# A decoder layer with a mixture of experts: a weight load of the third slot without its wait for the first gather

## The chip, the cores and the metric

The kernel runs on one core of a Trainium2 chip. The time is device microseconds of one execution: 581.81 us before, the median of 3 runs (579.86 to 581.87).

## What is computed

One decoder layer on 512 tokens of 1024 channels, in float32: an RMS norm and one input projection; a gated causal convolution (31 taps) beside block-sparse attention; an output projection; a hierarchical mixture of experts; a gate with per-layer embeddings, and a last norm. The part that matters here is the mixture. With x1 the state after the output projection:

```python
x = x + mixed @ w_out[i]                         # x1
g_idx = argmax(hf @ w_group + b_group)           # one of 4 groups for each token
top_vals, top_idx = top_k(e_logits, 2)           # two of its 8 experts
for e in range(32):
    hid = silu(h @ w_gate[e]) * (h @ w_up[e])    # 1024 -> 256
    y = y + gates[..., e:e + 1] * (hid @ w_down[e])
```

## The kernel before, in words

**Passes.** The 32 experts are worked in pairs, one pair to a pass. A pass takes 128 rows: 96 for its first expert (a = 0) and 32 for its second (a = 1). Passes 0 to 2 have fixed pairs (experts 2g and 2g + 1, `FIXED = 3`); the later ones are ordered by their number of tokens, which is known only after routing, and SyncE reads their experts' numbers from `order` in SBUF (`expert`, L579 to L583). GpSimd gathers a pass's rows from `rows_d` in DRAM into `xg` by an indirect DMA (L792 for passes 0 and 1, L772 for the others) and scatters its results to `y_d` (L786). Before that it stores the four quarters of the normed rows to `rows_d` (L761). In all its queue carries 4 stores, 17 gathers and 16 scatters. TensorE transposes the rows (`turn_tokens`, L1788), does the gate and up products (64 matmuls, L1800), transposes the hidden rows (L1813) and does the down products (32 matmuls, L1822). ScalarE and VectorE empty the banks in between (L968 to L981, L1371, L1449, L1454).

**Slots.** The weights of a pass are six loads of 1 MB: w_gate, w_up and w_down of each expert. There are three slots (`SLOTS = 3`): slots 0 and 1 lie in `wring`; slot 2 is put together from tiles that the earlier stages have given up: `mix` and parts of `arena` for gate and up, and, for the second expert's w_down, parts of the constants `c` and the tile `lnr`. Pass 3 would use slot 0 again; its first expert's gate and up are put "aside" in `xs`, the tile in which x1 was made, as soon as x1 is stored in DRAM (L686).

**SyncE's order around the change** (L619 to L695). All weight loads are issued by SyncE, on one queue, in the order of the program. Before and during the output projection it issues slot 0, most of slot 1 and parts of slot 2. After the last product of the output projection (`outc` 7) it loads the rest of slot 1, stores the last quarter of x1 (L650), and issues `load_one(2, 2, 0, 0)`, w_gate of slot 2's first expert. Then comes the wait for `gathered[0]`, the landing of pass 0's rows, then `load_one(2, 2, 1, 0)`, w_gate of slot 2's second expert, then the waits for the last root and for the logits' bank, and `load_split_rest(2)` into `lnr` (L609). Behind that stand the waits for the order ("owner"), for all stores of x1, and for the rows of the norm, and the two loads into `xs`. Then `reload` refills the slots: halves of gate and up after half of a pass's products (`half_up`, only for passes 0 and 1), the rest after `up_done`, w_down after `down_done`.

**TensorE around the first gather.** While VectorE works out the routing, TensorE runs filler transposes of the identity into a bank that nobody reads (`keep_busy`, L1732): 52, then 18, then 18. After the last 18 come `turn_tokens(0, 0, 0)`, which waits for `gathered[0]`, and pass 0. The gather itself waits for `tfirst`, the list of rows of passes 0 and 1 (L1348).

Of the kernel before, what the change touches and what calls it, by code (L numbers as in the profile page):

```python
# [215 lines left out]
def build(nc, x, w_in, w_out, w_r, w_gate, w_up, w_down, w_pg, w_pp, pT, b_pg, g_final, prm, cst, out):  # L216
    ctx = ExitStack()
    with ctx:
# [7 lines left out]
        def sem(name):  # L226
            return ctx.enter_context(nc.semaphore(name))
# [256 lines left out]
        gathered = [sem(f"gathered{s}") for s in range(2)]  # L484
# [47 lines left out]
        def _(sp):  # L532
# [52 lines left out]
            def load_one(w, n, a, i):  # L585
                sp.dma_start(up_w(w, a)[:, i],  # L586
                             (w_gate, w_up)[i][bass.ds(expert(n, a), 1)].rearrange("e (p k) n -> p (e k) n", k=DK)
                             ).then_inc(up_loaded[w], 16)
# [60 lines left out]
                banks.wait_emptied(sp, ("outc", 2 * TT - 2 + half))  # L649
            sp.dma_start(x1_rows[:, TT - 1], xs[:, TT - 1, :]).then_inc(x1_stored, 16)  # L650
            load_one(2, 2, 0, 0)
            sp.wait_ge(gathered[0], 16)
            load_one(2, 2, 1, 0)

            sp.wait_ge(root_ready, 4 * TT)
            banks.wait_emptied(sp, "logit")
            load_split_rest(2)
# [1260 lines left out]
```

## Time and profile before

| | |
|---|---|
| median of 3 runs | 581.81 us (579.86 to 581.87) |
| profiled execution, its own time | 579.72 us |
| its span | 577.9 us |
| mean granted TensorE clock | 0.958 |
| TensorE matmuls busy | 502.6 us (87%) |
| DMA read and written | 142.95 MB and 14.68 MB, 273 GB/s over the span |

A line is named as L586; a line can be that of a helper (`load_one` of SyncE is L586, whatever it loads, and a filler transpose is L1732). "SPq" is SyncE issuing DMAs; a DMA that is issued is not yet landed, and the time to landing stands apart. "A <- B" in a list of waits means that A's engine stood idle until B was done. In the windows, the DMA share is the mean busy share of the 16 DMA engines, and PEclk the TensorE clock granted, 1.00 being 2.4 GHz and 0.50 being 1.2 GHz.

### The profile page before, as it was taken

What the parts mean: (1) busy time and instruction counts of PE and PEld (TensorE: products, weight loads), DVE (VectorE), ACT (ScalarE), POOL (GpSimd) and SP (SyncE); (2) the same over time, 40 slices, a digit from 0 to 9 for tenths busy, and PEclk for the clock granted to TensorE, in tenths of its full rate; (3) what the DMA queues carried; (4) which work ended last, traced back from release to release, by engine and by line L of the source; (5) the groups of instructions that cost most, each with busy time, mean ns of one, the idle gap of its engine ahead of it and who ended that gap; (6) DMA issues with size and microseconds to landing.
All of it is one profiled execution on the core that took longest, in us unless ns stands there. A gap on an engine that the chain in (4) does not pass through costs nothing.

```text
span 577.9 us, 8877 instructions
## 1 busy us (share of the span) xinstructions
PE 502.6 (87%) x3227; PEld 298.8 (52%) x3227; DVE 295.7 (51%) x561; ACT 183.7 (32%) x351; POOL 78.5 (14%) x91
## 2 busy tenths in 40 slices
PE   3999999997879979988999996879868687999993
PEld 3788888774557658874333332223213222247882
DVE  4339899999996864487121111111101111166776
ACT  6821411337775353332011000000000000066764
POOL 1740000000032040010212221010111101010000
PEclk9999999999799999999999997997979899899998
DMA  9931300445506056498999999999999999868003
GB/s 315 372 134 39 113 15 16 149 159 170 218 1 273 1 216 258 160 388 306 356 410 416 419 418 421 417 419 420 380 412 409 387 375 414 341 223 317 0 9 139
DMA packets 38936, 150.33 MB, mean 260 GB/s; under 512 B 6000, under 2 KB 10608, under 8 KB 27888
## 3 DMA queue, kind: packets, MB, share of 16 engines
q1 hardware_dynamic: 33280, 139.14, 61.2%
q0 software_dynamic: 5328, 10.50, 5.0%
q8 instruction: 26, 0.43, 0.3%
q10 hardware_dynamic: 288, 0.15, 0.1%
q14 instruction: 14, 0.11, 0.1%
HBM read 142.95 MB, written 14.68 MB: 273 GB/s over the span
## 4 chain that ended last, share of the span: by engine, by line
PE 56%; SPq 15%; DMA 10%; DVE 9%; ACT 5%; issue 4%; POOL 1%; DVEq 0%; ACTq 0%; POOLq 0%
PE bank L1554 15%; PE bank L1800 10%; DMA wring<-w_up_in 8%; PE bank L1866 8%; SPq L586 7%; PE bank L1656 5%; PE bank L1822 4%; PE bank L1580 4%; SPq L514 3%; SPq L614 2%; PE bank L1845 2%; DMA wring<-w_in_in 2%; PE bank L1697 1%; DVE wring L1151 1%; DVE mix L1088 1%
## 5 line engine op out<-in xcount | busy, mean ns | idle before, releaser
L1800 PE MATMUL bank<-wring,arena 128*32 128x512 f32 x656 | 87.2, 657 | 20.7 <-DMA wring<-w_up_in 19.4
L1088 DVE SCALAR_TENSOR_TENSOR mix<-arena,pr,mix 128x512 f32<-128x512 f32 x120 | 86.6, 791 | 0.0
L1449 DVE TENSOR_TENSOR arena<-arena,bank 128x256 f32<-128x256 f32 x16 | 6.7, 420 | 139.1 <-ACT arena L975 139.1
L1800 PEld LDWEIGHTS bank<-wring,arena 128*32 128x32 f32 x656 | 25.0, 119 | 76.4 <-issue 71.1
L975 ACT ACTIVATE arena<-bank 128x256 f32<-128x256 f32 x16 | 6.2, 384 | 140.5 <-PE bank L1800 140.5
L1822 PE MATMUL bank<-wring,arena 128*32 128x512 f32 x352 | 40.0, 595 | 5.3 <-ACT arena L978 5.3
L1800 PE MATMUL bank<-mix,arena 128*32 128x512 f32 x240 | 37.7, 626 | 7.4 <-DMA arena<-w_up_in 7.4
L1454 DVE COPY arena<-bank 128x512 f32<-128x512 f32 x16 | 11.1, 692 | 53.7 <-PE bank L1822 53.7
L1800 PE MATMUL bank<-arena 128*32 128x512 f32 x80 | 37.6, 626 | 0.0
L1554 PE MATMUL bank<-hT_hi,win_hi 128*128 128x512 f32 x128 | 33.5, 398 | 2.1 <-DVE hT_lo L1066 1.5
L1554 PE MATMUL bank<-hT_lo,win_hi 128*128 128x512 f32 x128 | 31.6, 389 | 0.0
L1554 PE MATMUL bank<-hT_hi,win_lo 128*128 128x512 f32 x128 | 31.6, 389 | 0.0
L1554 PEld LDWEIGHTS bank<-hT_hi,win_hi 128*128 128x128 f32 x128 | 23.6, 188 | 10.3 <-ACT hT_hi L838 1.9
L981 ACT ACTIVATE arena<-bank 128x512 f32<-128x512 f32 x16 | 9.6, 597 | 60.8 <-PE bank L1822 60.8
L1800 PEld LDWEIGHTS bank<-mix,arena 128*32 128x32 f32 x240 | 10.7, 115 | 33.7 <-issue 31.6
L1554 PEld LDWEIGHTS bank<-hT_lo,win_hi 128*128 128x128 f32 x128 | 24.0, 188 | 5.0
L1554 PEld LDWEIGHTS bank<-hT_hi,win_lo 128*128 128x128 f32 x128 | 24.0, 188 | 5.0
L783 POOL COPY ycur<-tlist 128x1 int32 x16 | 2.9, 182 | 169.5 <-DVE arena L1454 169.5
L1822 PEld LDWEIGHTS bank<-wring,arena 128*32 128x32 f32 x352 | 10.3, 109 | 27.6 <-issue 20.5
L743 POOL TENSOR_TENSOR mixa_lo<-mix,mixa_hi 128x512 fp32r<-128x512 f32 x4 | 5.9, 1480 | 134.8 <-ACT mix L899 134.8
L1371 DVE TENSOR_TENSOR arena<-bank,pr 128x512 f32<-128x512 f32 x33 | 21.3, 686 | 2.0 <-PE bank L1788 1.9
L833 ACT ACTIVATE win_hi<-wring 128x1024 fp32r<-128x1024 f32 x20 | 20.0, 1070 | 6.3 <-DMA wring<-w_in_in 6.3
(262 smaller groups left out, 907.2 us busy)
## 6 DMA issues: line engine op xcount, KB each, us to landing
wring<-w_down_in SPq DMA_DIRECT2D x22, 1024.0 KB, 20.6
wring<-w_gate_in SPq DMA_DIRECT2D x18, 1024.0 KB, 16.1
wring<-w_up_in SPq DMA_DIRECT2D x18, 1024.0 KB, 19.9
wring<-w_in_in SPq DMA_DIRECT2D x3, 2048.0 KB, 14.4
arena<-w_down_in SPq DMA_DIRECT2D x5, 1024.0 KB
mix<-w_up_in SPq DMA_DIRECT2D x5, 1024.0 KB, 12.2
arena<-w_up_in SPq DMA_DIRECT2D x5, 1024.0 KB, 21.8
mix<-w_gate_in SPq DMA_DIRECT2D x5, 1024.0 KB, 17.4
```

The lines of the kernel that those rows point to most:

```text
L514: return eng.value_load(ap, min_val=least, max_val=most)
L586: sp.dma_start(up_w(w, a)[:, i], (w_gate, w_up)[i][bass.ds(expert(n, a), 1)].rearrange("e (p k) n -> p (e k) n", k=DK)).then_inc(up_loaded ...
L614: sp.dma_start(dn_w(w, a), src).then_inc(dn_loaded[w], 16)
L833: act.activation(win_hi[i][:, :, cols], win[i][:, :, cols], ACT.Copy).then_inc(win_hi_ready[i], 1)
L1088: ins = dve.scalar_tensor_tensor(out=mixc[:, mm, :], in0=u[:, mm, j:j + S], scalar=w, in1=mixc[:, mm, :], op0=ALU.mult, op1=ALU.add)
L1371: dve.tensor_tensor(xgT[:, s, 4 * kh:4 * kh + 4, :], pb[kh][:].rearrange("p (k n) -> p k n", k=4), pr[:, Q_FFN + 4 * kh:Q_FFN + 4 * kh + 4 ...
L1554: ins = pe.matmul(bk(name)[:], w[:, k, m * P:(m + 1) * P], h[:, k, :], start=(j == 0 and k == 0), stop=(j == 2 and k == DK - 1))
L1580: ins = pe.matmul(bk(("v", t))[:], h[:, k, t * P:(t + 1) * P], w[:, k, :], start=(j == 0 and k == 0), stop=(j == 2 and k == DK - 1))
L1656: ins = pe.matmul(bk(name)[:], src[:, m, t * P:(t + 1) * P], weight[:, m, half * 512:(half + 1) * 512], start=(j == 0), stop=(j == 3 * CM ...
L1800: ins = pe.matmul(pb[2 + s][lo:hi, :], xgT[:, s, k, lo:hi], weights[:, :, k, :], start=(k == 0), stop=(k == DK - 1))
L1822: ins = pe.matmul(pb[6 + half][lo:hi, :], hidT[:, s, k, lo:hi], dn_cols(w, a, k, half), start=(k == 0), stop=(k == FK - 1))
L1866: ins = pe.matmul(bk(name)[:], lhs, w[:, k, :], start=(j == 0 and k == 0), stop=(j == 2 and k == DK - 1))
```

## The change

SyncE no longer waits for pass 0's rows ahead of w_gate of slot 2's second expert. All else stays.

```diff
             sp.dma_start(x1_rows[:, TT - 1], xs[:, TT - 1, :]).then_inc(x1_stored, 16)
             load_one(2, 2, 0, 0)
-            sp.wait_ge(gathered[0], 16)
             load_one(2, 2, 1, 0)
-
             sp.wait_ge(root_ready, 4 * TT)
             banks.wait_emptied(sp, "logit")
             load_split_rest(2)
```

## Rows read from the trace of the kernel before

**Rows 1.** Chain that ended last, 240 to 300: start us, us, what.

```profile
258.69 3.37 PE bank L1732 x18
...
262.05 1.41 PE bank L1788 x8
...
264.68 7.07 PE bank L1800 x64
```

**Rows 2.** GpSimd's timeline at the first gather, then line L792 in 258 to 259.

```profile
258.09 1.07 POOL L792 DMA_INDIRECT arena<-rows_d,tfirst  x1 [10.53 <-DVE tfirst L1348]
...
DMA to landing us min/median/max: 3.7/3.7/3.7
```

**Rows 3.** SyncE's waits, 240 to 283: us in total, times, longest.

```profile
SPq L586 <- DMA arena<-rows_d,tfirst: 17.2, 1, 17.2
```

**Rows 4.** SyncE's timeline, 240 to 283: start us, us, what.

```profile
243.75 0.43 SPq L650 DMA_DIRECT2D x_d<-xs  x1
...
244.23 0.43 SPq L586 DMA_DIRECT2D mix<-w_gate_in  x1
...
261.84 0.33 SPq L586 DMA_DIRECT2D arena<-w_gate_in  x1
...
262.27 0.41 SPq L609 DMA_DIRECT2D lnr<-w_down_in  x1
...
263.94 0.35 SPq L686 DMA_DIRECT2D xs<-w_gate_in  x1
...
265.07 0.34 SPq L686 DMA_DIRECT2D xs<-w_up_in  x1
...
278.63 1.44 SPq L614 DMA_DIRECT2D wring<-w_down_in  x2
```

**Rows 5.** Windows: us, busy by engine, PEclk, DMA share, GB/s.

```profile
242.00:258.00 16.00, 13.57 (x133) 12.71 (x132) 10.98 (x48) 7.59 (x9) 0.53 (x1) 1.00 1.01 389
...
259.50:263.00 3.50, 3.50 (x19) 3.28 (x18) 2.93 (x13) 0.00 (x0) 0.98 (x1) 0.51 0.44 123
...
278.00:279.00 1.00, 1.00 (x16) 0.37 (x12) 0.54 (x1) 0.45 (x1) 0.04 (x1) 1.00 0.65 262
...
282.00:350.00 68.00, 64.82 (x580) 22.39 (x576) 14.40 (x28) 7.59 (x17) 13.19 (x21) 1.00 1.02 412
```

**Rows 6.** Line L650, the last store of x1 (issued at 243.75).

```profile
DMA to landing us min/median/max: 15.5/15.5/15.5
```

**Rows 7.** VectorE's timeline, 257 to 260.

```profile
258.46 0.17 DVE L1358 CAST order<-bank 1x32 int32<-1x32 f32 x1
```

**Rows 8.** Line L786 in 280 to 281, then in 290 to 500; last, L772 in 275 to 276.

```profile
L786 POOL DMA_INDIRECT y_d<-arena,ycur x1: 1011/1011/1011, 280.2 to 280.2; - x1
...
DMA to landing us min/median/max: 7.9/7.9/7.9
...
DMA to landing us min/median/max: 7.7/8.5/9.1
...
L772 POOL DMA_INDIRECT arena<-rows_d,tcur x1: 1017/1017/1017, 275.2 to 275.2; - x1
...
DMA to landing us min/median/max: 6.2/6.2/6.2
```

**Rows 9.** TensorE's timeline, after two pauses, and the window of the first.

```profile
458.78 9.79 PE L1800 MATMUL bank<-wring,arena 128*32 128x512 f32 x64 [3.95 <-DMA wring<-w_up_in]
...
490.98 8.77 PE L1800 MATMUL bank<-wring,arena 128*32 128x512 f32 x64 [2.95 <-DMA wring<-w_up_in]
...
458.50:464.00 5.50, 5.22 (x28) 1.48 (x32) 0.00 (x0) 0.00 (x0) 1.02 (x1) 0.50 1.00 414
```

**Rows 10.** Part 3 of the page, DMA queues.

```profile
q1 hardware_dynamic: 33280, 139.14, 61.2%
...
q0 software_dynamic: 5328, 10.50, 5.0%
```

## The prediction

> **What bounds the kernel now.** I read the chain of waits first, then SyncE's waits and issues around the changed line, then what the first gather and the DMA engines do there, and last how TensorE behaves after a pause. The profiled execution spans 577.9 us and took 579.72 us, 2.1 us under the median of 581.81; the sum is made against it, and its difference is then put on 581.81.
>
> The chain goes through the place where the removed wait sits. TensorE runs its last 18 filler transposes up to 262.05 and goes straight on to the transposes of pass 0's rows (L1788), then to its 64 gate and up products at 264.68, which take 7.07 us [rows 1]. So pass 0 lies on the path, and so do its rows. The first gather is issued at 258.09 and lands 3.7 us later, at 261.8 [rows 2]: only 0.25 us before the filler ends. There is no other slack: a gather that lands later than 262.05 delays pass 0 by the difference.
>
> SyncE stands in the removed wait for 17.2 us, "SPq L586 <- DMA arena<-rows_d,tfirst" [rows 3], and then issues four loads: w_gate of slot 2's second expert at 261.84, the end of that expert's w_down into `lnr` at 262.27, and the two loads into `xs` (w_gate and w_up of pass 3's first expert) at 263.94 and 265.07 [rows 4]. Nobody on the chain waits for any of them: pass 2 and pass 3 come much later, and the chain names TensorE for passes 0 and 1. What the wait does buy is in the windows: the DMA engines are full up to 258 (389 GB/s), and in 259.5 to 263 they move 123 GB/s at a share of 0.44 [rows 5]. That is the two gathers, nearly alone.
>
> **The change, part by part.** (1) One wait instruction goes from SyncE: nothing on any path by itself.
>
> (2) The w_gate load of 1.05 MB (1024 KB) moves from 261.84 to right behind the one issued at 244.23, so about 244.7. The 0.26 MB for `lnr` follows as soon as the logits are read. Neither has a register to read, since pass 2 is one of the fixed ones. The DMA queue is full there, so they move no byte earlier than the end of that queue. Before, the queue's last load is the one of 244.23. The x1 store ahead of it lands 15.5 us after 243.75, at 259.25 [rows 4, 6]; behind it come the 1.05 MB, 2.5 us at the 412 GB/s of the full stretch [rows 5]. With the two loads added, 1.31 MB / 412 GB/s = 3.2 us more of full queue lie behind them, just where the gather starts moving (258.09 plus its own 1.07 us of issue = 259.16 [rows 2]).
>
> (3) The two loads into `xs` are no longer held by the rows. They need the order, which VectorE writes at 258.46 [rows 7], and all x1 stores, the last of which lands at 259.25. Before, 1.26 us passed between the end of the `lnr` issue (262.68) and the first of them (263.94) [rows 4], for the waits, already met, and the register reads. So they go out at about 260.4 and 261.5, 3.5 us earlier, 2.1 MB more. Together with (2) SyncE's queue is then full through the whole life of both gathers.
>
> (4) What a gather costs under a full queue. The trace has it later: the scatter issued at 280.2, the same kind of transfer from the same queue, with nothing of GpSimd's ahead of it, between 2 MB of w_down issued from 278.63 and the loads after, lands after 7.9 us. The 14 later scatters take 7.7 to 9.1 us, median 8.5. The gather of 275.2, whose neighbours ran out on the way (share 0.65 in 278 to 279), took 6.2 us [rows 5, 8]. I take 7.9 us, since the load standing beside that one, 1 to 2 MB ahead and 1 MB coming, is closest; bounds are 3.7 us (no harm at all) and 9.1 us. Rows at 258.09 + 7.9 = 265.99 instead of 261.8, so pass 0 begins 265.99 - 262.05 = **3.9 us** later. The second gather, needed only after pass 0's products, stays hidden: even 9.1 us and 3 us more behind the first end before the 271.7 + 3.9 at which it is asked for.
>
> (5) TensorE now stands idle from 262.05 to 266.0. After pauses of 3.95 and 2.95 us before 458.78 and 490.98 the 64 products took 9.79 and 8.77 us instead of 7.07, and the granted clock was 0.50 (1.2 GHz of 2.4) in 458.5 to 464 [rows 1, 9]. Work at half clock loses half of its time, so 2 x (9.79 - 7.07) = 5.4 us and 2 x 1.7 = 3.4 us of these products ran at the low level. The transposes run at half clock before as well (0.51 in 259.5 to 263 [rows 5]) and cost nothing new. The products start 264.68 - 262.05 = 2.6 us after the transposes, so with the same stretches counted from the transposes 0.8 to 2.8 us of the products run low, cost 0.4 to 1.4; I take **0.9 us**. Bounds: 0, if the clock is high by then, and 2.7 us, the full price of 458.78.
>
> (6) Is any of it given back? By 278 to 279 the queue has run down before as well (share 0.65), and it fills again for good only with the w_down loads at 278.63, which wait for pass 0's last product. From 282 on it is full (1.02) [rows 4, 5]. So the bytes moved early only lengthen the pause before that point, and the start of the full stretch, on which both the TensorE part up to 350 and the DMA part behind it hang, moves with pass 0. Nothing comes back: gain 0, cover the pause at 278.
>
> Sum: 3.9 + 0.9 = **4.8 us** later, 579.7 + 4.8 = 584.5 for the profiled execution, 581.8 + 4.8 = **586.6 us** for the median. Bounds within this case: low, the gather at 6.2 us (264.3, 2.2 us late, no cost of clock), 584.0; high, 9.1 us (5.1 late) and 2.7 of clock, 589.6.
>
> **Rivals.** *A: the gather takes its turns and hardly suffers.* SyncE's queue moved 139.14 MB in 33280 packets, 4.2 KB each; GpSimd's queue 5328 packets over its 37 transfers, 144 each, 9 on each of 16 engines [rows 10]. One packet of 4.2 KB on one of 16 engines takes 4.2 KB x 16 / 412 GB/s = 0.16 us. If each packet of the gather waits for just one such, it loses 9 x 0.16 = 1.5 us, lands at 263.3 and costs 1.2 us: 583.0, no change. Against it stand the scatters of [rows 8], which lose over 4 us to 3.7 with that very traffic; for it, that the queue might be shorter at 259 than I think. The Trainium skill ("DMA: Bandwidth & Descriptors", Queues, rings and completion order) says that each DMA engine goes round robin between its queue rows, packet by packet, which is this mechanism; by that rule alone the time would be 583.0, while the trace's scatters speak against it being all. Chance 0.19.
>
> *B: faster.* The pause of 259.5 to 263 is filled with 1.31 MB that are then not in the later full stretch: 3.2 us less if the gather still lands by 262.05 and the queue never runs empty between 263 and 282. That gives 578.6, just over 0.5% less. It decides from the point where the bytes saved exceed the pause at 278; the share of 0.65 there is against it, as is [rows 8]. Chance 0.05.
>
> **How the numbers follow.** 0.5%, 2.9 us, is about what a measurement of this kernel can tell from no change. My case, a late gather, has 0.76, of which its low end (gather 6.2 us, under 2.9 us in all) falls within 0.5%: some 0.05. So faster 0.05, same 0.19 + 0.05 = 0.24, slower 0.71. The range takes in rival A's 583.0 with a little below it for the scatter of runs (579.86 to 581.87), and goes up to the high bound: 582 to 590.
>
> **What would show it.** In the profile after: the SyncE row for the wait gone, w_gate issued near 244.7 and the `xs` loads at 260 to 261; DMA share near 1.0 in 259.5 to 263 where it was 0.44; the first gather 7 to 9 us to landing instead of 3.7; a wait "PE L1788 <- DMA arena<-rows_d" of about 4 us; the granted clock low into pass 0's 64 products and these over 7.07 us; all later passes shifted by the same 4 to 5 us; DMA share well under 0.65 near 275 to 283. A gather that lands within 5.5 us makes me wrong towards A. Later passes that are shifted by less than pass 0 make step 6 wrong, and a shift that shrinks through the full stretch would be B's.

## The result, and the profile after

The changed kernel takes **586.62 us** (median of 5 runs, 585.4 to 587.69) against 581.81 us: slower, ratio 1.0091 with the 95% interval 1.0064 to 1.0117, so by 3.7 to 6.8 us. The profiled execution took 585.49 us, its span is 583.7 us against 577.9. Lines of the changed kernel are two lower than before behind the change: L1786 is L1788 of before, L1798 is L1800, L790 is L792.

SyncE's timeline of the changed kernel, start and duration in us:

```profile
245.91 0.44 SPq L586 DMA_DIRECT2D mix<-w_gate_in  x1
246.39 0.44 SPq L586 DMA_DIRECT2D arena<-w_gate_in  x1
248.88 0.33 SPq L609 DMA_DIRECT2D lnr<-w_down_in  x1
261.82 0.35 SPq L684 DMA_DIRECT2D xs<-w_gate_in  x1
262.96 0.34 SPq L684 DMA_DIRECT2D xs<-w_up_in  x1
284.56 1.44 SPq L614 DMA_DIRECT2D wring<-w_down_in  x2
```

The wait of 17.2 us is gone, and w_gate for `arena` leaves right behind the one for `mix`, where [rows 4] have it 17.6 us later. The rows that the change does not touch are 1.5 to 1.7 us later too (the `mix` load at 245.91 against 244.23, the first gather's issue at 259.57 against 258.09), and that is no effect of the change: it arises at 213, ahead of every instruction that it moves. The chain of before and then of after:

```profile
213.78 3.92 PE bank L1656 x16
```

```profile
213.39 5.79 PE bank L1654 x16
```

The same 16 matmuls began 0.4 us earlier and took 1.9 us more, since the granted clock was at its low level for a moment (0.50 in 212 to 215, where it was 1.00 before); that leaves 1.5 us. Two single executions differ by such things; so below, times inside a profile are counted from the issue of the first gather, 258.09 before and 259.57 after. In the chain of after this stretch reads:

```profile
259.57 6.45 DMA arena<-rows_d,tfirst
...
266.06 1.98 PE bank L1786 x8
...
269.26 8.42 PE bank L1798 x64
```

The chain now leads through the gather: 6.45 us to landing instead of 3.7 [rows 2]. The transposes of pass 0's rows begin 6.49 us after the issue (before 262.05 - 258.09 = 3.96), and the 64 products end 18.11 us after it (before 13.66, [rows 1, 2]): **4.4 us** later. TensorE's timeline gives the pause, and the windows the reason and the clock (columns as in [rows 5]):

```profile
266.06 1.97 PE L1786 MATMUL bank<-c,arena 128*128 128x128 f32 x8 [3.71 <-DMA arena<-rows_d,tfirst]
```

```profile
259.50:263.00 3.50, 2.40 (x20) 2.05 (x20) 3.15 (x13) 0.00 (x0) 2.08 (x2) 1.00 0.99 419
265.50:272.00 6.50, 4.70 (x24) 2.34 (x28) 3.66 (x15) 2.43 (x5) 0.00 (x0) 0.50 0.72 300
270.00:275.00 5.00, 5.00 (x44) 1.38 (x40) 4.79 (x12) 0.51 (x1) 0.00 (x0) 0.80 0.06 26
288.00:350.00 62.00, 59.40 (x531) 20.24 (x526) 12.71 (x25) 6.83 (x15) 12.16 (x20) 1.00 1.02 411
```

While the gather is under way the DMA engines are full: share 0.99 and 419 GB/s, where [rows 5] show 0.44 and 123. In 270 to 275 they stand nearly still, 0.06: all that was moved early is done, and the next loads wait for pass 0. From 288 on they are as full as before, only later. The two w_down loads that wait for pass 0's last product, and that open the full stretch, go out at 284.56 instead of 278.63 [rows 4]: 5.9 us later, the 1.5 us of chance and 4.4 us of the change. The two passes of [rows 9], whose 64 products began at 458.78 and 490.98, have them now, by the chain of after, at:

```profile
465.02 7.11 PE bank L1798 x64
...
497.25 7.07 PE bank L1798 x64
```

That is 6.2 and 6.3 us later. Both wait for a load of w_up here as they did before, so their beginnings show how far the DMA queue is behind. Their ends do not: the clock was high here (1.00), the products took 7.11 and 7.07 us instead of 9.79 and 8.77, and by their ends the shift is only 3.6 and 4.6 us. The span is 5.8 us longer: 1.5 us of chance at 213 and 4.3 us from the gather on (583.7 - 259.57 against 577.9 - 258.09).

### The profile page after: what moved, and what is told of

Its sections match the earlier page's. It is cut to its first block, busy times and chain, and to the rows that moved or that the text cites. A ratio compares the mean times of both kernels' runs of the same rounds, so it can differ in the third digit from the quotient of the medians.

```text
span 583.7 us, 8877 instructions
## 1 busy us (share of the span) xinstructions
PE 507.3 (87%) x3227; PEld 301.3 (52%) x3227; DVE 295.8 (51%) x561; ACT 183.6 (31%) x351; POOL 77.8 (13%) x91
## 4 chain that ended last, share of the span: by engine, by line
PE 53%; SPq 15%; DMA 12%; DVE 9%; ACT 5%; issue 4%; POOL 1%; DVEq 0%; POOLq 0%; ACTq 0%
PE bank L1552 15%; PE bank L1798 10%; DMA wring<-w_up_in 9%; PE bank L1864 8%; SPq L586 7%; PE bank L1654 5%; PE bank L1820 4%; PE bank L1578 4%; SPq L514 3%; SPq L614 2%; PE bank L1695 1%; PE bank L1622 1%; DVE wring L1149 1%; DMA arena<-rows_d,tfirst 1%; DMA wring<-y_d 1%
## 5 line engine op out<-in xcount | busy, mean ns | idle before, releaser
L1798 PE MATMUL bank<-wring,arena 128*32 128x512 f32 x656 | 87.2, 657 | 17.6 <-DMA wring<-w_up_in 16.3
L1798 PEld LDWEIGHTS bank<-wring,arena 128*32 128x32 f32 x656 | 25.3, 119 | 73.2 <-issue 70.4
L1798 PE MATMUL bank<-mix,arena 128*32 128x512 f32 x240 | 39.7, 653 | 8.5 <-DMA arena<-w_up_in 8.5
L1798 PE MATMUL bank<-arena 128*32 128x512 f32 x80 | 39.6, 653 | 0.0
L1798 PEld LDWEIGHTS bank<-mix,arena 128*32 128x32 f32 x240 | 11.2, 119 | 36.1 <-issue 31.3
L1786 PEld LDWEIGHTS bank<-c,arena 128*128 128x128 f32 x136 | 15.3, 145 | 16.5 <-issue 12.6
```

What stands on the lines that cost most here:

```text
L1786: ins = pe.transpose(pb[k // 4][:, k % 4 * P:(k % 4 + 1) * P], xg[:, s, k * P:(k + 1) * P], ident)
L1798: ins = pe.matmul(pb[2 + s][lo:hi, :], xgT[:, s, k, lo:hi], weights[:, :, k, :], start=(k == 0), stop=(k == DK - 1))
```

## The experiments

The kernel before ran beside each set on the same chip, with a median of 580.65 to 581.25 us; ratios are to those runs.

**1. Which of the loads does it?** The change lets 1.31 MB go early and the two loads into `xs` after them. First, the 1.31 MB alone:

```diff
             load_one(2, 2, 0, 0)
-            sp.wait_ge(gathered[0], 16)
             load_one(2, 2, 1, 0)
             ...
             load_split_rest(2)
+            sp.wait_ge(gathered[0], 16)
```

> Only the w_gate and lnr loads (1.31 MB) go early; the two loads into xs now stand behind the wait for the first gather. Theory (any full SyncE queue slows the gather): 3.2 us more of queue stand in front of the gather, so it lands 5.5 to 6.5 us after its issue instead of 3.7, pass 0 starts 2 to 3 us late, the clock costs 0 to 1 us: 2 to 3.5 us slower than before, 583.8 to 585.3. Rival (the loads into xs, issued while the gather is under way, do the harm): the time of before, 581.8, gather at 4 us.

Measured: 585.77 us against 580.75, ratio 1.0097 (1.0069 to 1.0125). The chain of this kernel:

```profile
260.02 6.43 DMA arena<-rows_d,tfirst
```

The gather takes as long as in the full change, and the time is slower by as much: 4.0 to 7.3 us, above the 2 to 3.5 that the theory gave this half. As far as the times can tell, it is the whole. The other half, `xs` loads ahead of the wait and the rest behind it:

```diff
             load_one(2, 2, 0, 0)
-            sp.wait_ge(gathered[0], 16)
-            load_one(2, 2, 1, 0)
             sp.wait_ge(root_ready, 4 * TT)
             banks.wait_emptied(sp, "logit")
-            load_split_rest(2)
             ...
                              ).then_inc(aside_loaded, 16)
+            sp.wait_ge(gathered[0], 16)
+            load_one(2, 2, 1, 0)
+            load_split_rest(2)
```

> The other half: the loads into xs go out as soon as the order is known and x1 is stored (about 260.4), the w_gate and lnr loads stand behind the wait for the first gather, after them. Theory: SyncE's queue is empty from about 259.5 until the first xs load's data comes, by when the first gather is nearly done: it lands after 3.7 to 4.5 us and the time is that of before, 581.8 to 582.5. Rival (the loads into xs do the harm): gather near 6.5 us, time near that of the change, 586.6.

Measured: 580.66 us against 580.75, ratio 1.0003 (0.9980 to 1.0027). SyncE's timeline and the chain of this kernel:

```profile
261.18 0.36 SPq L682 DMA_DIRECT2D xs<-w_gate_in  x1
```

```profile
258.83 3.73 DMA arena<-rows_d,tfirst
```

The loads leave 2.35 us after the gather's issue and are too late to hurt the first gather. (The second takes 5.7 us here, against 4.5 before, and nobody waits for it.) The rival falls: by themselves, these loads do no harm that can be measured.

**2. How much queue, and does it matter which load?** Two smaller doses. Only `lnr` early, with w_gate behind the wait:

```diff
-            sp.wait_ge(gathered[0], 16)
-            load_one(2, 2, 1, 0)
-
             sp.wait_ge(root_ready, 4 * TT)
             banks.wait_emptied(sp, "logit")
             load_split_rest(2)
+            sp.wait_ge(gathered[0], 16)
+            load_one(2, 2, 1, 0)
```

> Only the 0.26 MB for lnr go early, w_gate stays behind the wait. Theory (the harm grows with the queue that stands before the gather; 0.26 MB / 412 GB/s = 0.6 us): gather 4.0 to 4.6 us, pass 0 late by 0.2 to 0.8 us, time 0 to 0.8 us above before. Rival (any transfer in the queue costs the full 2.7 us): gather 6.4 us, 4 to 5 us slower.

Measured: 583.25 us against 580.65, ratio 1.0030 (0.9997 to 1.0062), its runs wide apart (578.93 to 587.34). The median is 2.6 us slower, where the theory said 0 to 0.8 and the rival 4 to 5, and the time alone leaves it unclear. The gather speaks for the theory's 4.0 to 4.6:

```profile
258.11 4.55 DMA arena<-rows_d,tfirst
```

And only w_gate early, the wait now right ahead of the `lnr` load:

```diff
-            sp.wait_ge(gathered[0], 16)
             load_one(2, 2, 1, 0)
 
             sp.wait_ge(root_ready, 4 * TT)
             banks.wait_emptied(sp, "logit")
+            sp.wait_ge(gathered[0], 16)
             load_split_rest(2)
```

> Only w_gate (1.05 MB) goes early; lnr and the loads into xs stay behind the wait. Theory (2.5 us more of queue, of a gather that takes 6.4 us in a queue that does not end): gather 5.6 to 6.3 us, pass 0 1.5 to 2.3 us late and a pause of TensorE of 2 to 3 us, in which the clock may or may not fall: 2 to 4.5 us slower than before. Rival (harm in proportion to bytes, 1.05 of 1.31 MB): 4 us slower.

Measured: 584.94 us against 580.65, ratio 1.0080 (1.0057 to 1.0102), 3.3 to 5.9 us, which fits the upper end of the theory and the rival's 4 us alike. The chain tells more, a gather of 6.44 us, slightly over the theory's figure:

```profile
259.16 6.44 DMA arena<-rows_d,tfirst
```

Together, one execution each: 3.7 to 4.2 us with the queue of before in front of the gather (3.7 in the kernel before and with the `xs` loads early, 3.8 and 4.1 in experiments 4 and 5, 4.2 in the last one of this group), 4.55 with 0.26 MB more, 6.44 with 1.05 MB, 6.43 with 1.31 MB, 6.45 with those and the `xs` loads. So a longer queue means a later gather, and harm in proportion to the bytes is not seen between 1.05 and 1.31 MB; the first small dose stands only 0.3 us above the spread of equal queues.

One thing orders all these figures better than the bytes do: when the load that stands last in front of the gather lands. In the w_gate experiment this load, its issue and then the landings of its line, where the longest is its own:

```profile
245.86 0.44 SPq L586 DMA_DIRECT2D arena<-w_gate_in  x1
...
DMA to landing us min/median/max: 17.6/18.6/19.6
```

It lands at 245.86 + 19.6 = 265.5, and the gather at 265.6. The same holds wherever the queue ends with one of these loads:

| kernel | last load in front lands | gather lands |
|---|---|---|
| before | 261.6 | 261.8 |
| `lnr` early | 262.5 | 262.7 |
| w_gate early | 265.5 | 265.6 |
| w_gate early, w_down back (below) | 263.6 | 263.7 |

In experiments 1 (second half), 4 and 5 the gather follows the last load by 0.1 to 0.2 us too. With both loads in front (the change, the first half of experiment 1 and experiment 3), the gather lands 0.2 to 0.3 us behind w_gate and 0.5 to 0.7 us ahead of `lnr`; in the change w_gate lands at 246.39 + 19.3 = 265.7, the gather at 266.0, and `lnr` at 248.88 + 17.8 = 266.7. So the harm stops growing at the end of the w_gate load. Why the gather keeps this company is not shown: the traces do not tell whether its rows arrive so late or only the signal that they have landed.

In the other direction, the w_gate load ahead of the wait goes behind it as well:

```diff
-            load_one(2, 2, 0, 0)
             sp.wait_ge(gathered[0], 16)
+            load_one(2, 2, 0, 0)
             load_one(2, 2, 1, 0)
```

> The kernel before with the w_gate load of slot 2's first expert (1.05 MB, issued at 244.2 before) moved behind the wait as well: the queue ends 2.5 us sooner, ahead of the gather's issue. Theory: the gather already met an almost empty queue, so it lands 3.2 to 3.7 us after issue, TensorE's filler holds pass 0 where the clock is low in it, and the time is that of before within 0.3%; at most 0.5 us is won. Rival (the gather of before is already slowed by the queue's end): gather under 3 us, 0.5 to 1 us faster. The extra 1.05 MB fill the pause of 262 to 268; if they do not fit in it, up to 1 us slower.

Measured: 580.84 us against 580.65, ratio 1.0006 (0.9988 to 1.0023). The gather lands 0.3 us sooner than before and 2.2 us behind the last transfer in front of it, the store of x1 (243.72 + 15.6 = 259.3), so 3.4 us is what it needs with nothing in its way; the rival's figure of under 3 us is not reached. Nothing comes of the 0.3 us: pass 0's transposes start 0.5 us sooner and take 0.5 us longer (1.91 instead of 1.41), with the clock at 0.50, and the products begin at 264.69 as before. The other megabyte that now lies in the pause costs nothing that can be measured. The gather's line of this kernel, us from issue to landing:

```profile
DMA to landing us min/median/max: 3.4/3.4/3.4
```

Last, the same w_gate load early, but another megabyte taken out of the queue for it:

```diff
-            for a in range(2):
-                load_down(1, 1, a)
+            load_down(1, 1, 0)
             ...
             load_one(2, 2, 0, 0)
-            sp.wait_ge(gathered[0], 16)
             load_one(2, 2, 1, 0)
-
+            sp.wait_ge(gathered[0], 16)
+            load_down(1, 1, 1)
```

> w_gate of slot 2's second expert goes early as in the change, but another megabyte, w_down of slot 1's second expert, goes behind the wait in its place (as does lnr): the queue in front of the gather is as long as before, 5.5 MB, with other bytes in it. Theory (it is the length of the queue at the gather, not which load or which tile it goes to): gather 3.4 to 4.5 us, the time of before within 0.3%. Rival (this load itself harms, by its tile in arena next to the one that the gather fills): gather near 6.4 us and 4 us slower.

Measured: 582.09 us against 581.25, ratio 1.0022 (0.9999 to 1.0044): at most 2.6 us, where the rival wants 4, and not told apart from no change. The chain of this kernel:

```profile
259.49 4.24 DMA arena<-rows_d,tfirst
```

So it is neither this load nor its tile; it is how long the queue in front of the gather lasts.

**3. What is the clock's part?** The changed kernel with more filler in front of pass 0:

```diff
-            keep_busy(18)
+            keep_busy(40)
             def lists():
```

> The changed kernel with 40 filler transposes before pass 0 instead of 18, so that TensorE is busy until about 265 (22 x 0.12 us more at full clock) while it waits for the gather. Theory (1.9 us of the loss are the clock: products 8.42 instead of 7.07 us, transposes 1.97 instead of about 1.1 to 1.4): the clock stays at 1.00, the products take 7.07 us, 1.5 to 1.9 us less than the changed kernel, 584.7 to 585.1. If the filler itself falls into a low stretch it ends after the gather and costs 1 to 2 us instead. Rival (the clock is only a bystander): 586.6, whatever the products take.

Measured: 584.4 us against 580.75, ratio 1.0072 (1.0048 to 1.0096). Against the 1.0091 of the change that is 0.2% or 1.1 us back, with intervals that overlap: by the times alone unclear. Its chain:

```profile
258.43 6.25 PE bank L1730 x40
...
266.78 7.07 PE bank L1798 x64
```

The gather is slow here too (6.4 us from 257.84), yet the products run at full clock, 7.07 us, and end 16.0 us after the gather's issue, against 18.1 with 18 transposes: 2.1 us less in this execution. The transposes took 0.89 us instead of 1.98 and the products 1.35 us less, that is 2.4 us of clock, less 0.35 us by which the transposes start later after the gather's issue. So the clock's share is real: 2.4 us against a full clock, and 1.9 us against the kernel before, whose own transposes ran partly low (1.41 us). The filler fell into a low stretch in this one (0.56 in 259.5 to 263), took 6.25 us (4.58 at full clock, in the next experiment), and ended just behind the gather. This execution was the fastest of ten (581.01 us, up to 587.49); where the low stretch falls otherwise the filler may end later and cost time, which would explain that the median gains less, but no trace shows it.

**4. Does a late pass 0 arrive at the end by itself?** The kernel before, wait in place, with the same 40 transposes:

```diff
-            keep_busy(18)
+            keep_busy(40)
             def lists():
```

> The kernel before, wait in place, with 40 filler transposes instead of 18: pass 0 is late by TensorE's own doing, no load is moved and the gather meets an empty queue. Theory (step 6: whatever delays pass 0 arrives at the end undiminished): pass 0 starts 1.5 us (clock high) to 3 us (clock low at first) later, and the span grows by the same, 583.3 to 584.8; gather still 3.7 us. Rival (the DMA-bound stretch has slack that swallows a late start, and the change costs by its traffic): 581.8.

Measured: 582.93 us against 580.75, ratio 1.0044 (1.0026 to 1.0061), 2.2 us slower with no load moved and a gather of 3.8 us, within the 1.5 to 3 us expected. The rival, slack that swallows the delay, falls. In the profiled execution the filler ran at full clock (4.58 us from 261.33) and pass 0's products end 14.3 us after the gather's issue, only 0.7 us later than before; the median's 2.2 us is more than this one execution shows, and no trace tells why. One to one is therefore not measured by this run; that a delay made by TensorE alone costs time is.

**5. Are the early bytes worth anything?** The kernel before with its loads held back further:

```diff
             sp.wait_ge(gathered[0], 16)
+            sp.wait_ge(gathered[1], 16)
             load_one(2, 2, 1, 0)
```

> The kernel before with a second wait behind the first, for the other gather too: the four loads go out some 2 us later still than before. Theory (step 6: none of these loads is needed before pass 2, and their bytes are carried in a stretch that is not full): the time of before within 0.3%; the second gather may land a little sooner, which nobody waits for. Rival B turned round (bytes moved towards the full stretch cost time there, up to the 2 us by which they are late): 1 to 2 us slower than before.

Measured: 580.77 us against 580.65, ratio 0.9997 (0.9976 to 1.0018). SyncE's timeline of this kernel:

```profile
263.47 0.33 SPq L586 DMA_DIRECT2D arena<-w_gate_in  x1
```

That is 5.7 us after the gather's issue (257.78), where [rows 2, 4] have 261.84 - 258.09 = 3.75. So 3.4 MB that go out 2 us later cost nothing that can be measured (at most 1.0 us by the interval).

No version beat the kernel before.

## Why the prediction was right

The number, 586.6 us, was met, and that it was met so closely is luck: two terms erred in opposite directions. The mechanism, a late gather and a low clock behind it, was right.

- **Steps 1 to 3, what moves where**: right. Less the 1.5 us of chance, w_gate left at 244.9 (said: 244.7) and the `xs` loads at 260.3 and 261.5 (said: 260.4 and 261.5). But step 3's remark that these loads help to keep the queue full gave them a part that they don't have: experiment 1 puts all the harm on the 1.31 MB.
- **Step 4, the gather under a full queue**: mechanism right, size wrong. Said 7.9 us to landing and pass 0 late by 3.9 us; measured 6.45 and 6.49 - 3.96 = 2.5 us. The announced sign of 7 to 9 us did not come. The failing choice is the row: I took the scatter of 280.2 (writes to DRAM, 7.9 us) and passed over the gather of 275.2 at 6.2 us [rows 8], nearly the 6.4 us of four kernels. The reason given for the choice was also misread: the scatter did have a transfer of GpSimd's ahead of it, since that gather landed only at 275.2 + 6.2 = 281.4. Which of these makes the scatter slower, its direction, that neighbour or the load beside it, no run separates; and since the gather of 275.2 had a queue that ran out beside it, its fitting value may be chance too.
- **Step 5, the clock**: mechanism right, size too small. Said 0.9 us; measured 1.9: the transposes took 1.98 us instead of 1.41, and the products 8.42 instead of 7.07. The low level lasted from the pause until 272, 5.9 us after the work came back at 266.06, while I had counted on 3.4 to 5.4 [rows 9] and had priced the transposes at nothing. Those of before had run low as well in [rows 1], but only in part (1.41 us, where 0.89 is full clock).
- **Step 6, nothing given back**: nothing speaks against it, but it is less sharply measured than the rest. The DMA engines stand still in 270 to 275, the opening of the full stretch moves by just as much as pass 0, and experiment 5 finds the loads' date worthless. The time from the gather's issue to the end of the span is 4.3 us longer for a pass 0 that ends its products 4.4 us later, but a single one is a rough measure: in the six kernels whose products end 13.5 to 14.0 us after the issue it goes from 318.6 to 322.4 us, with a mean of 320.6. The three kernels with products 18.1 to 18.2 us after it have 322.7 to 324.1, mean 323.5, that is 2.9 us more. Their medians, 4.3 to 5.0 us above the kernel before, are the size of the whole delay, with intervals of 3.3 to 5.9, 3.7 to 6.8 and 4.0 to 7.3 us. One sign failed: the DMA share near 275 to 283 was to be well under 0.65; it was 0.42 in 274 to 278 but 0.83 to 0.91 in 278 to 284. The pause lay earlier, in 270 to 275, and the refills behind pass 0 came after it.
- **Rival A**, fair turns, lay on the right side in the direction and at half of the price: 1.5 us by one packet's wait per packet of the gather, 2.7 us measured and 3.0 from the 3.4 us with the shorter queue. A gather that lands within 5.5 us would have spoken for it; it took 6.45. The turns that the Trainium skill describes ("DMA: Bandwidth & Descriptors", Queues, rings and completion order) would agree with a harm that does not grow from 1.05 to 1.31 MB; at the price of one packet per turn the rule's time of 583.0 is below the measured interval, and turns at that price would not make the gather land together with the last load in front of it. What each packet waits for was not measured by itself.
- **Rival B**, faster, failed at its first condition, the gather on time. The second half of experiment 1 meets that condition in part (its `xs` loads are early and the gather is on time), and it is not faster either.

The sum, as measured: 2.5 + 1.9 = 4.4 us for 3.9 + 0.9 = 4.8 us.

## What to carry to other kernels

A wait that no data needs can still be a gate: before taking it out, look for a short transfer on the path that will then share the DMA engines with what it held back, and ask whether the held bytes are scarce at that point. Look up when the load in front of the short transfer lands: here the gather landed right behind it. Add the clock of TensorE for the pause that it causes. Where a load must go early, take an equal load out of the queue for it: in this kernel it is how long the queue in front of the short transfer lasts that decides, not which bytes are in it.

## What the runs showed of the hardware

- The same gather (same rows, 1.07 us of it GpSimd's issue) lands 3.4 us after its issue when the last transfer in front of it, there the store of x1, has landed 2.2 us earlier, after 3.7 to 4.2 us behind the queue of before, 4.55 with 0.26 MB more, and 6.4 with 1.05 MB or more. In ten of the eleven profiles it landed within 0.4 us after a load that stood in front of it: the last one, or w_gate where `lnr` came behind. The prediction had no such rule.
- A load's landing is later than the end of its traffic: in the kernel before, the last load in front of the gather lands at 244.23 + 17.4 = 261.6, while the DMA share is 0.44 from 259.5 on [rows 5].
- With no instruction changed there, the granted clock fell somewhere in 209 to 218 in 7 of the 11 profiles (among them the changed kernel, not the one before). In five of the seven it was 0.50 through all of 212 to 215, and these five issue the first gather at 259.16 to 260.74; the six others do so at 257.78 to 258.83. The 18 filler transposes took 2.2 us where the clock was full throughout and up to 3.63 us where it was low. That is why single executions are compared here from a common event on.
